# A two-block transformer kernel on one core: moving VectorE's low parts in the convolutions, and the order of work around the last norm

## What is computed

```python
def long_conv_bidir(u, h_fwd, h_bwd, bias):
    ...
    U = jnp.fft.rfft(u.astype(jnp.float32), n=2 * L, axis=1)
    K = jnp.fft.rfft(k2, n=2 * L, axis=0)
    y = jnp.fft.irfft(U * K[None], n=2 * L, axis=1)[:, :L]
    return (y + u.astype(jnp.float32) * bias.astype(jnp.float32)).astype(u.dtype)

def hyena_mixer(...):
    ...
    for n in range(HY_ORDER):            # HY_ORDER = 2
        z = gates[n] * long_conv_bidir(z, filt[:, 0, n], filt[:, 1, n], bias[n])
    return z

def gated_merge(g_na, g_hy, y_na, y_hy, w_na_o, w_hy_o, w_out):
    m = jax.nn.sigmoid(g_na) * (y_na @ w_na_o) + jax.nn.sigmoid(g_hy) * (y_hy @ w_hy_o)
    return m @ w_out

def second_block(...):
    ...
        x = x + g1 * gated_merge(gna, ghy, y_na, y_hy, w_na_o[i], w_hy_o[i], w_out[i])
        h2 = modulate(rmsnorm(x, norm2_g[i]), sh2, sc2)
        x = x + g2 * swiglu(h2, ffn_w1[i], ffn_w3[i], ffn_w2[i])
    return rmsnorm(x, final_g)
```

## Time and profile before

| | us |
|---|---|
| median of 3 runs | 1658.41 |
| lowest and highest | 1656.42, 1660.17 |
| the profiled execution | 1653.27 |
| its span in the trace | 1651.4 |
| TensorE busy | 1583.5 |
| VectorE, ScalarE, GpSimd busy | 1012.0, 698.2, 419.1 |
| mean granted clock of TensorE | 0.989 of full |

### The profile page before, as it was taken

One profiled execution on the slowest core, in us unless ns is written; L12 is line 12 of the kernel. 1 busy time (PEld: TensorE's weight loads), 2 busy tenths in 40 slices (PEclk: granted clock), 3 DMA queues, 4 the chain that ended last, 5 costly groups with the idle time before them and its releaser, 6 DMA issues. The chain is left out here.

```text
span 1651.4 us, 21244 instructions
## 1 busy us (share of the span) xinstructions
PE 1583.5 (96%) x8600; PEld 1329.5 (81%) x8600; DVE 1012.0 (61%) x1443; ACT 698.2 (42%) x1012; POOL 419.1 (25%) x350
## 2 busy tenths in 40 slices
PE   5999998999999999999999999999799999999997
PEld 5778876677878888788888778887687899999886
DVE  6675545657987587433875643346963688886324
ACT  5644335554533243322532334444443644443222
POOL 0024302330621011100062012223442455551002
PEclk9999999999999999999999999999999999999999
DMA  7342212344244345322436423224444033324221
GB/s 295 103 141 90 77 34 102 102 158 167 102 175 156 128 169 189 128 78 101 151 120 244 133 75 114 89 86 129 163 145 176 26 107 112 113 106 151 80 77 51
DMA packets 47068, 203.93 MB, mean 123 GB/s; under 512 B 14352, under 2 KB 14736, under 8 KB 28346
## 3 DMA queue, kind: packets, MB, share of 16 engines
q1 hardware_dynamic: 37346, 171.84, 29.0%
q0 software_dynamic: 9088, 30.38, 5.4%
q10 hardware_dynamic: 536, 0.35, 0.1%
HBM read 181.56 MB, written 21.00 MB: 123 GB/s over the span
## 5 line engine op out<-in xcount | busy, mean ns | idle before, releaser
L559 PE MATMUL ps<-xh,whi 128*128 128x512 f32 (+1 forms) x1136 | 402.0, 354 | 7.3 <-DVE wlo L1807 5.5
L561 PE MATMUL ps<-xh,wlo 128*128 128x512 f32 (+1 forms) x1136 | 397.7, 350 | 0.0
L560 PE MATMUL ps<-xl,whi 128*128 128x512 f32 (+1 forms) x1136 | 396.4, 349 | 0.0
L1807 DVE TENSOR_TENSOR wlo<-raw,whi 128x2048 fp32r<-128x2048 f32 x92 | 228.8, 2488 | 139.8 <-ACT whi L1191 139.7
L1191 ACT ACTIVATE whi<-raw 128x512 fp32r<-128x512 f32 (+1 forms) x190 | 236.1, 1247 | 150.3 <-PE ps L561 103.1
L559 PEld LDWEIGHTS ps<-xh,whi 128*128 128x128 f32 x1136 | 215.6, 190 | 47.5 <-issue 12.6
L561 PEld LDWEIGHTS ps<-xh,wlo 128*128 128x128 f32 x1136 | 214.4, 189 | 29.8
L560 PEld LDWEIGHTS ps<-xl,whi 128*128 128x128 f32 x1136 | 214.8, 189 | 28.6
L2230 DVE SCALAR_TENSOR_TENSOR xr<-ps,pc,xr 128x511 f32<-128x511 f32 x88 | 65.2, 747 | 41.8 <-ACT xr L1191 40.2
L2641 POOL TENSOR_TENSOR act<-xr 128x512 f32<-128x512 f32 x22 | 38.9, 1768 | 201.4 <-DVE xr L2230 200.7
L2539 DVE TENSOR_TENSOR wlo<-raw,whi 128x512 fp32r<-128x512 f32 x98 | 77.6, 823 | 0.4 <-ACT whi L1191 0.4
(11 more groups left out here) (455 smaller groups left out, 3529.5 us busy)
## 6 DMA issues: line engine op xcount, KB each, us to landing
raw<-in_w_in SPq DMA_DIRECT2D x35, 1024.0 KB, 5.0
raw<-in_ffn_w SPq DMA_DIRECT2D x33, 1024.0 KB, 4.8
raw<-in_ada SPq DMA_DIRECT2D x24, 1024.0 KB, 4.8
raw<-in_w_up SPq DMA_DIRECT2D x22, 1024.0 KB, 4.9
raw<-in_w_down SPq DMA_DIRECT2D x11, 1024.0 KB, 4.8
xd<-X POOLq DMA_DIRECT2D x8, 512.0 KB, 7.9
td<-vr POOLq DMA_DIRECT2D x16, 256.0 KB, 3.7
raw<-td SPq DMA_DIRECT2D x4, 1024.0 KB, 5.5
```

What stands on the lines that cost most here:

```text
L559: pe.e.matmul(o, lh, rh, start=start, stop=False)
L560: pe.e.matmul(o, lh, rl, start=False, stop=False)
L561: return pe.e.matmul(o, ll, rh, start=False, stop=stop)
L1807: up(ve.e.tensor_tensor(lo, raw[conv_at[j] % 3][:, :], hi.bitcast(F32), ALU.subtract), "wlo")
```

## The change

Nothing is computed otherwise; instructions change places, one changes engine, and one small one is added.

In the convolutions: the first two of the four `first_low` stand between the second and third product of t = 1. The low parts of tiles 79 and 80 leave this place. Tile 79's now stands behind the last `sums_low` of n = 1, and tile 80's behind the last `last_low`, at the start of the merge. SyncE asks for two weight tiles fewer between its loads for the sums, and for them later.

In the last norm: the transposes of t = 2 go behind the second and those of t = 3 behind the third feed-forward tile of c = 0. The last gated sum (t = 3, second half) goes from GpSimd to VectorE. ScalarE starts with a square root of a constant, which loads the table. ScalarE does the squares of t = 2 and 3 behind channels 15 and the high part of tile 88. VectorE takes out tiles 0 and 1 before their two inversions. GpSimd's eight adds wait for all four token tiles' low parts. Quarters 0 and 1 go in front of the sums' splits, quarters 2 and 3 behind them, and in front of the silu. The whole tiles of n = 0 take banks 2 and 3, which the transposes of t = 2 used.

```diff
@@ tensor
-                if t == 3:
-                    last_norm_rows(2)
...
-                       xh4, xl4, 36, lambda c, i: last_norm_rows(3) if (c, i) == (0, 1) else None)
+                       xh4, xl4, 36, lambda c, i: last_norm_rows(i + 1) if (c, i) in ((0, 1), (0, 2)) else None)
...
-                                            ("f_s", FS[f"silu{p2}", n])))
+                                            ("f_s", FS[f"silu{p2}", n])), None if n else "channels")
@@ scalar
+            act(ss_b, eps[:, 1:2], ACT.Sqrt)
             for t in range(2):
                 rows_3(t)
                 rows_2(t, 6)
-            rows_3(2)
             channels(14)
-            rows_2(2, 6)
             channels(15)
             high(J_UP2 + 1)
+            rows_3(2)
             rows_3(3)
+            rows_2(2, 6)
             rows_2(3, 6)
...
+            fast_high(0)
+            fast_high(1)
             rows_sum(5, 13)
             rows_sum(6, 15)
-            fast_high(0)
-            fast_high(1)
...
             rows_sum(3, 16)
+            fast_high(2)
+            fast_high(3)
@@ vector
                 sums_low(n, 3)
+                if n:
+                    low_parts(J_MERGE)
...
                         up(ve.e.tensor_tensor(tq[a][:, :], b[:, :], x1[:, i, :], ALU.mult), "hz")
+                        if t and q == 1:
+                            first_low(0)
+                            first_low(1)
                 if n == 0:
-                    for k in range(4):
-                        first_low(k)
+                    first_low(2)
+                    first_low(3)
...
-                if n == 0:
-                    low_parts(J_MERGE + 1)
...
+            def last_gated_sum():
+
+                x = X[:, 3, 512:1024]
+                ve.wait_ge(sig["gr_m"], 8)
+                ve.wait_ge(sig["gr_x"], 7)
+                ve.wait_ge(sig["x3"], 48)
+                up(ve.e.tensor_tensor(x, x, tq[0][:, :], ALU.add), "gr_x")
+
+            out_rows(0)
+            out_rows(1)
+            root(6)
+            root(7)
             out_rows(2)
             channels(14)
-            root(8)
             channels(15)
             out_rows(3)
+            last_gated_sum()
+            root(8)
+            low_parts(J_UP2 + 1)
             root(9)
-            low_parts(J_UP2 + 1)
@@ gpsimd
-                for t in range(4):
+                for t in range(4 - cg):
                     gated_sum(t, cg, 4 * cg + t + 1, tq[(4 * cg + t) % 7][:, :])

+            po.wait_ge(sig["ch_lo"], 36)
             for t in range(2):
-                po.wait_ge(sig["ch_lo"], 34 + 2 * t)
@@ sync
-                    weights(conv_at[J_MERGE + 1] + 3)
+                    weights(conv_at[J_MERGE + 1] + 1)
```

More of the change, by code:

```diff
@@ L57 @@
 POOLS = {"all": range(8), "dense": range(5), "beside": range(5, 8), "first": range(4, 8),
-         "gates": range(2), "attention": range(2, 8)}
+         "gates": range(2), "attention": range(2, 8), "channels": range(2, 4)}
 class Fills:
@@ L1746, in scalar_program @@
                 act(yg[:, 512 * m:512 * m + 512], b[:, :], ACT.Silu, "f_s")
-            for q in range(2, 7):
+            for q in range(4, 7):
                 fast_high(q)
@@ L2512, in out_rows @@
                 gated_part(tile(("wout", t, 1)), tq[(4 + t) % 7][:, :], 1)
-            for t in range(2):
-                out_rows(t)
-                root(6 + t)
+            def last_gated_sum():
[8 more added lines that the diff above has]
+            root(7)
             out_rows(2)
             channels(14)
-            root(8)
             channels(15)
             out_rows(3)
+            last_gated_sum()
+            root(8)
+            low_parts(J_UP2 + 1)
             root(9)
-            low_parts(J_UP2 + 1)
             channels(16)
@@ L2539, in fast_low @@
                 up(ve.e.tensor_tensor(lo, product_source(n, p), hi.bitcast(F32), ALU.subtract), "wlo")
+            fast_low(0)
+            fast_low(1)
             rows_sum(0, 5)
             rows_sum(1, 6)
-            fast_low(0)
-            fast_low(1)
             ve.wait_ge(sig["ch_hi"], 39)
@@ L2547, in vector_program @@
             rows_sum(3, 3)
+            fast_low(2)
+            fast_low(3)
             for m in range(2):
@@ L2551, in vector_program @@
                 up(ve.e.tensor_tensor(act2[:, m, :], b[:, :], yg[:, 512 * m:512 * m + 512], ALU.mult), "f_a")
-            for q in range(2, 6):
+            for q in range(4, 6):
                 fast_low(q)
```

## The result

The changed kernel takes 1654.20 us (median of 20 executions, 1648.05 to 1657.68), the kernel before 1657.14 us (20 executions, 1651.53 to 1660.89). The ratio of the two is 0.9977, with a 95% interval of 0.9966 to 0.9988: faster by 0.23%, between 2.0 and 5.6 us. The profiled execution took 1649.03 us with a span of 1647.2 us, where before it was 1651.4.

The account below looks back on a forecast made before the run. TensorE, busy 96% of the span, bounds the kernel; only its idle and half-clock stretches can be won. Convolutions -2.3 and last norm -3.5 sum to -5.8 us: 1652.6 us median, range 1649 to 1656.5, with rivals 1647.5 to 1657.5.

Parts of the forecast that it names:

- Interleaved low parts: First convolution: two low parts between VectorE's products let TensorE begin 1.1 us earlier, with a later wait up to 0.4 us.
- The chain as a block: Second convolution: VectorE's 18.2 us chain from first products to end of sums starts and ends 2.3 us earlier.
- The clock behind the 2.3 us wait: Convolutions: half clock still follows the shortened wait for xrr (2.4 us); if not, another 1.6 us at most is saved.
- part A: The convolutions' edits together: -2.3 us, bounds -1.0 and -3.3.
- The moved weights' low parts: Two weights' low parts, 2 x 2.25 us, move behind the sums and into the merge; nothing of it on the path.
- Norm: Last norm: 0.75 and 2.38 us waits go, a new 0.5 us wait comes; feed-forward's second half begins 4.7 us earlier.
- table and order: Last norm: early table load and VectorE's two tiles first remove the 0.75 us wait; third product tile at 1277.9, not 1278.8.
- The give-back: Before the second whole tile: GpSimd's adds start no earlier, slowed low parts behind them make a 1.6 us wait, was 0.60.
- the second rival: VectorE's chain behind the adds slowed throughout: 4.8 us wait plus 1.7 us half clock, total -1.0 us, 1657.4; 17%.
- part B: The last norm's edits together: -3.5 us, bounds -5.2 (no wait) and +1.3.
- The first, no new wait: Everything hidden: convolutions win 3.3 us, last norm 5.2 us, giving 1649.9 us; 24%.
- the third: GpSimd's adds themselves slowed to 2.28 us each, ending 6 us later; total +5.0 us, 1663.4; 4%.

Follow-up runs that it names:

- no_interleave: The changed kernel with all four first_low again behind the four gate products, the weights' low parts still moved; convolutions 63.58 us, 521.1 us from yn's transposes, one execution.
- the eight traces: One trace each of the eight kernels with the convolutions' change whole and no filling of TensorE's waits there; convolutions 61.25 us once, 62.7 to 62.8 five times, 64.0 twice.
- adds_early: The changed kernel with GpSimd's eight adds again waiting for the first three token tiles only; 518.3 us from yn's transposes, one execution.
- root_back: The changed kernel without the early square-root table load and with VectorE's first inversion again ahead of its second product tile; norm 22.04 us, 522.6 us from yn's transposes, one execution.
- pool_holds: The changed kernel, with GpSimd's first sums of weights waiting until the fourth quarter's low part is made; ratio to the kernel before 0.9962, median 1651.09 us.
- quarters_first: The changed kernel with quarters 2 and 3 made ahead of xrr and clr on ScalarE and VectorE; ratio to the kernel before 0.9970, median 1650.75 us.
- norm_only: The changed kernel with the convolutions' edits undone; ratio to the kernel before 0.9993, 520.8 us from yn's transposes.

## Why the prediction was right, and where its steps were not

The time lies in the range, and the direction is right. The size is not: 5.8 us were forecast, and the medians differ by 2.9, the ratio by 3.8 (2.0 to 5.6), the traces by 3.4 from the transposes of yn on. The range helped: 1647.5 to 1657.5 us also holds the kernel before, 1657.14. So did the base: before's median came out 1.3 us under the 1658.41 that I started from.

- **Interleaved low parts.** Forecast 1.1 us earlier, less a wait of up to 0.4 us if the clock stays up. TensorE began 1.16 us earlier (1161.32 - 1159.30 - 0.86), and the later wait was 0.88 us: the two low parts took 2.38 us beside GpSimd, not the 1.3 I reckoned with, and pushed the last product. no_interleave puts the net at 0.94.
- **The chain as a block.** Right: VectorE's first products came 2.09 us earlier in the stretch, and its last low part 2.1.
- **The clock behind the 2.3 us wait.** I took it to fall, since it had behind 2.38 us. It stayed at 1.00 in the changed kernel and in five more of the eight traces. By my own working A should then have been 3.3 us. It was 2.07, because the seven groups behind the wait took 6.72 us at full clock (1159.30 to 1166.02) where I had 4.9 and 0.4 of wait: they waited 1.9 us in all for late low parts. In adds_early and root_back the clock did fall there, and they took 6.73. So the clock at this place is worth nothing either way, and that the 2.3 came out near is luck. The failing step lies further on: I priced the clock only behind the longest wait, and not behind the chain's last ones, where no wait hides it. That is 1.46 us in seven of the eight traces named above; the changed kernel's is the eighth. By the mean of the eight, part A is worth 0.4 us and not 2.3.
- **The moved weights' low parts.** Right. Both are made under cover (1184.41 and 1195.05), and the merge takes the same 83.6 us.
- **Norm.** Forecast -4.7, measured -5.06. The wait of 0.5 us is 0.27; table and order bring 0.98.
- **The give-back.** The mechanism and its place are as forecast; the term was mis-sized. I slowed xrr to 2.3 us and gave the other low parts 1 us more together; clr took 2.30 and the quarters 2.35, which is 2.2 us more. The wait is 2.79 us in place of 1.6. Behind it is a misreading of the earlier trace rows: I took the 1.34 us at 1308.89 as a low part that GpSimd leaves alone. It stood beside the adds for 0.25 us only, they end at 1309.14, and it slowed GpSimd's next operation in its turn (2.28 us). So it does not speak against the rule that I had held it against. I also kept half clock behind it for the second rival, which starts from a wait of 4.8. A wait of 2.8 is enough, and it costs 1.48 us. So part B is -1.29, not -3.5. That the adds would start no earlier I had right, but took as given: it is the change's own wait that holds them, and without it the three stretches are 3.3 us shorter (adds_early).
- **The rivals.** The first, no new wait, is refuted for this kernel, but pool_holds and quarters_first have it built in: 4.5 us more. The second had the right two terms and too large a wait. In the third the adds would be slowed; they took 12.33 us where they had taken 12.29.

## What to carry to other kernels

When the engine that sets the end gets ahead, look at once at the chain that did not move with it, here eight adds on GpSimd, held by the change's own wait, and the low parts behind them: it takes back what it doesn't share. Before ordering VectorE's and GpSimd's work beside each other, price each with both busy (here up to 1.1 us on every VectorE operation, so short ones suffer most), and hold back the one that nobody waits for. A wait of TensorE costs its length and, behind those of 2.79 us here and mostly behind a row of three shorter ones, about 1.5 us of half clock on top; where that falls on the path, cheap work in the wait buys it back. One trace does not tell how a kernel's clock usually goes: the first trace of the changed kernel was the one of eight without the fall.

## What the runs showed of the hardware

- VectorE and GpSimd slow each other when VectorE's operation reads two tiles in SBUF: 1024 elements take 1.21 us undisturbed and 2.30 beside GpSimd, 512 elements 0.68 and 1.75 to 1.78; GpSimd's `ts<-raw` takes 1.30 and 2.29. The one that has begun keeps its time and the other ends about its own plain time behind it (s and `ts<-raw` at 1306.45 and 1306.66, xrr and clr behind them). `act<-ps,xr` beside `ts<-raw` slowed neither.
- TensorE's granted clock fell to its lower level during or behind waits of 2.38 us (two of two traces), 2.79 to 2.81 (five of five), 3.44 (three of three) and 4.20 (one). At 2.64 and 2.65 us it fell in before and not in norm_only; at 2.14 to 2.29 us in two of the eight traces named above.
- In seven of these eight it also fell behind the three waits of 1.52, 1.60 and 1.66 us. The same waits in the changed kernel's trace left it at 1.00. I have not settled what decides between them.
- Transposes of a 128x128 identity during the waits kept the clock at 1.00 there in all three kernels that had them, one trace each.
